# A hosted modulation sum is moved from the first projection phase to the second (fused two-block transformer step)

## What is computed

```python
mod = jax.nn.silu(c) @ w_mod[l] + b_mod[l]
sh1, sc1, ga1, sh2, sc2, ga2 = jnp.split(mod[:, None, :], N_MOD, axis=-1)
p_lat = modulate(rmsnorm(x, g_pre_mix[l]), sh1, sc1) @ w_in[l]
p_ctx = modulate(rmsnorm(ctx, g_pre_mix[l]), csh1, csc1) @ w_in[l]
...
x = x + ga1 * rmsnorm(y_lat, g_post_mix[l])
h_lat = modulate(rmsnorm(x, g_pre_ffn[l]), sh2, sc2)
```

## Time and profile before

| | |
|---|---|
| median of 3 runs | 3192.8 us (3184.38 to 3198.31) |
| span of the profiled execution | 3181.1 us |
| PE busy | 3001.6 us (94%) |
| DVE busy | 2101.7 us (66%) |
| ACT busy | 1289.5 us (41%) |
| POOL busy | 136.9 us (4%) |
| DMA, mean | 185 GB/s |
| first phase's 32 units | about 206 to 358 us |
| differential attention | 361.6 to about 432 us |
| second phase | about 433 to 728 us |

### The profile page before, as it was taken

How to read it: one execution, slowest core, us unless ns; L and a number is a source line. 1 busy time by engine, 2 the same in 40 slices (tenths; PEclk the granted TensorE clock), 3 DMA queues, 4 the chain that set the end, 5 groups by cost and what they waited for, 6 DMA issues and landing times. The chain is left out here.

```text
span 3181.1 us, 42696 instructions
## 1 busy us (share of the span) xinstructions
PE 3001.6 (94%) x16505; PEld 2496.0 (78%) x16505; DVE 2101.7 (66%) x3030; ACT 1289.5 (41%) x2138; POOL 136.9 (4%) x200
## 2 busy tenths in 40 slices
PE   5999889999989999999998999998999999998997
PEld 2577658888779999998887888876757878886766
DVE  5768645746768789887876669545735744774355
ACT  6642334526444444444344323215334224344243
POOL 1000000001010000000001000000010000000000
PEclk9999999999999999999998999999999999999999
DMA  8867224751667777777784546640512644682333
GB/s 269 272 227 270 90 81 140 259 204 35 232 206 259 251 246 258 242 237 271 262 290 155 175 133 201 206 162 14 185 66 100 206 140 139 217 286 73 106 107 138
DMA packets 255577, 589.24 MB, mean 185 GB/s; under 512 B 21977, under 2 KB 30401, under 8 KB 251024
## 3 DMA queue, kind: packets, MB, share of 16 engines
q1 hardware_dynamic: 246336, 546.64, 52.2%
q0 software_dynamic: 8640, 39.22, 3.5%
q10 hardware_dynamic: 400, 0.66, 0.1%
HBM read 571.72 MB, written 14.72 MB: 184 GB/s over the span
## 5 line engine op out<-in xcount | busy, mean ns | idle before, releaser
L2725 DVE TENSOR_TENSOR w_lo<-raw,w_hi 128x1024 fp32r<-128x1024 f32 (+1 forms) x732 | 860.9, 1191 | 395.6 <-ACT w_hi L2704 381.3
L2704 ACT ACTIVATE w_hi<-raw 128x1024 fp32r<-128x1024 f32 (+1 forms) x732 | 741.5, 1032 | 908.1 <-PE bank L2775 514.5
L696 DVE SCALAR_TENSOR_TENSOR acc<-raw,sc_t,acc 128x1024 f32<-128x1024 f32 x480 | 600.9, 1279 | 36.1 <-DMA acc<-in_b_ada 16.1
L2783 PE MATMUL bank<-f_hT_hi,w_hi 128*128 128x256 f32 x1408 | 400.3, 284 | 0.9 <-DVE w_lo L2725 0.9
L2773 PE MATMUL bank<-w_hi,l_hT_hi 128*128 128x512 f32 (+1 forms) x1056 | 391.5, 371 | 8.5 <-DVE w_lo L2725 8.4
L2784 PE MATMUL bank<-f_hT_lo,w_hi 128*128 128x256 f32 x1408 | 399.1, 283 | 0.0
L2785 PE MATMUL bank<-f_hT_hi,w_lo 128*128 128x256 f32 x1408 | 399.1, 283 | 0.0
L2774 PE MATMUL bank<-w_lo,l_hT_hi 128*128 128x512 f32 (+1 forms) x1056 | 388.0, 367 | 0.0
L2775 PE MATMUL bank<-w_hi,l_hT_lo 128*128 128x512 f32 (+1 forms) x1056 | 387.9, 367 | 0.0
L2783 PEld LDWEIGHTS bank<-f_hT_hi,w_hi 128*128 128x128 f32 x1408 | 270.9, 192 | 2.8 <-issue 1.7
L2785 PEld LDWEIGHTS bank<-f_hT_hi,w_lo 128*128 128x128 f32 x1408 | 271.0, 192 | 0.0
(11 more groups left out here) (436 smaller groups left out, 4653.2 us busy)
## 6 DMA issues: line engine op xcount, KB each, us to landing
raw<-in_w_in SPq DMA_DIRECT2D x240, 512.0 KB, 4.9
raw<-in_w_mod SPq DMA_DIRECT2D x192, 512.0 KB, 5.0
raw<-in_w_ada SPq DMA_DIRECT2D x192, 512.0 KB, 4.6
raw<-in_w_up SPq DMA_DIRECT2D x176, 512.0 KB, 4.8
raw<-in_w_out SPq DMA_DIRECT2D x96, 512.0 KB, 5.0
raw<-in_w_down SPq DMA_DIRECT2D x88, 512.0 KB, 5.3
raw<-in_w_in SPq DMA_DIRECT2D x32, 288.0 KB, 3.2
raw<-in_w_ukv SPq DMA_DIRECT2D x16, 512.0 KB, 4.0
```

What stands on the lines that cost most here:

```text
L696: e.scalar_tensor_tensor(acc[a][:, :], raw[s % RAW_SLOTS][:, :], scalar, acc[a][:, :], ALU.mult, ALU.add).then_inc(fma_done, 1)
L2704: e.activation(slot(w_hi[u % SPLIT_SLOTS], g.width), slot(raw[s % RAW_SLOTS], g.width), ACT.Copy).then_inc(hi_ready, 1)
L2725: e.tensor_tensor(slot(w_lo[u % SPLIT_SLOTS], g.width), slot(raw[s % RAW_SLOTS], g.width), slot(w_hi[u % SPLIT_SLOTS], g.width).bitcast(F3 ...
L2783: e.matmul(o, hi[:, kk, c], xh[:, k, 0:n], start=first, stop=False)
```

## The change

One sum group, the first half of `sh2`, leaves the first phase's list and joins the second's. With it the positions of all hosted steps of the two phases change.

```diff
-        gemms([dq1, dk1] + gs[4:6], sums_mix + sums_ffn[0:1], hosts=[(8, 7), (15, 8), (23, 8)], side=(dk_group, drope_dve, 1), then=rows_out, start=start, hooks=hooks)
+        gemms([dq1, dk1] + gs[4:6], sums_mix, hosts=[(9, 10), (20, 11)], side=(dk_group, drope_dve, 1), then=rows_out, start=start, hooks=hooks)
...
-        gemms([mg, mk0, mo0, mk1, mo1, mq0, mq1, mv0, mv1], sums_ffn[1:3], hosts=[(26, 28), (56, 9)],
+        gemms([mg, mk0, mo0, mk1, mo1, mq0, mq1, mv0, mv1], sums_ffn[0:3], hosts=[(10, 20), (32, 16), (52, 14)],
               first=gd_pool, hooks=gates_hooks)
```

## The result

The changed kernel takes 3194.65 us (median of 20 runs, 3191.78 to 3200.8), the kernel before 3188.68 (20 runs, 3180.81 to 3198.31). The ratio is 1.0020 with a 95% interval of 1.0013 to 1.0027: **slower, by some 6.4 us** (the medians differ by 6.0). A second series gave 1.0022 (1.0013 to 1.0031). The profiled execution became 9.4 us longer, 3190.5 against 3181.1.

A forecast was written before the change was run, and what follows sets the result against it. PE was taken to bound both phases. The terms -1.5 + 3.0 - 1.0 + 1.8 + 5.6 + 3.0 - 0.3 gave +10.6 us, from a median of 3192.8 to 3203.4 us; range 3191 to 3215.

The forecast's parts named there:

- The closing one: Whole kernel: the forecast rise of 0.33% lies within the 0.5% (16 us) that a measurement can't tell from no change.
- One stated sign of being wrong: Start of the attention stage: starting earlier than 361.6 us would show the forecast wrong.
- Part 1: Phase 1: 16 sum steps removed relieve DVE, and PE's three listed waits go; -1.5 us, bounds 0 and 2.
- Part 2: Phase 1's end: the barrier waits for the gate rows' stores to land, +3.0 us; row's PE work leaves mid-phase, -1.0.
- Part 3: Phase 2: one more turn of 16 small matmuls on PE between units, with no wait; +1.84 us.
- Part 4: Phase 2, mk0's end: earlier evacuation makes PE wait 3.9 us, then 1.7 us lost at half clock; +5.6 us.
- Part 5: Phase 2, mo1 and mq0: added sum steps make DVE late, +3.0 us in five short waits; -0.3 at mq0's end.
- (a): Rival: mk0's evacuation is hidden after all, so the sum is +5.0, 3197.8 us; chance 0.17.
- (b): Rival: DVE becomes the outright bound of mo1 and mq0, sum 17.3, 3210.1 us; chance 0.18.
- (c): Rival: phase 1 is held by DVE and loads, so removing 16 steps gives -7.1, 3185.7 us; chance 0.05.
- (d): Rival: the placement does nothing measurable anywhere, tail hidden too; -1.0, 3191.8 us; chance 0.05.

The follow-up runs named there:

- e1: The changed kernel with mk0's evacuation put back before weight unit u20, counted in weight units, not list positions; 3188.82 us, ratio 0.9994 to the kernel before.
- e7: The kernel before with mk0's evacuation before weight unit u18 and its later parts one unit sooner than in e3; 3191.48 us, ratio 1.0015.
- e3: The kernel before with only mk0's evacuation moved ahead, to before weight unit u18, hosts as before; ratio 1.0002 to the kernel before.
- e2: e1 with mk1's evacuation put before weight unit u36 too; 3186.2 us, ratio 0.9985 to the kernel before.
- e5: e2 with phase 2's hosted sum steps behind u9-u23, u24-u35 and u56-u64, none in mq0 and mq1; ratio 0.9964, then 0.9977 to the kernel before.
- e4: The changed kernel without POOL's wait for the gate rows' stores at the first phase's end; ACT waits in the attention instead; ratio 1.0012 to the kernel before.

## Why the prediction was wrong

The text called 10.6 us up, and put this within the 0.5% that a measurement can't tell from no change. The time went up by 6.4 us, and with 20 runs the interval excludes "no change". The direction of the sum and the places of its terms were right. Two steps failed. The closing one, that a difference of 0.33% can't be measured, was wrong. And the sum was two thirds too high: the landing of the stores was put too long, the first phase's relief too small and the attention at nothing, while the half clock in mo0 was put too short. The last of these errors has the opposite sign of the others; that it took back 1.7 us of them is luck. One stated sign of being wrong also came true: the attention starts earlier than 361.6, at 358.58. Of these 3.0 us, 1.1 lie in the start part that wasn't changed, and 1.9 are the first phase's -3.4 and +1.5 where the text had -2.5 and +3.0.

- **What can be told.** I took 0.5% from the spread of single runs (3184 to 3198). The interval of the ratio is +-0.07%. A forecast of +0.33% should have been called slower. The forecast time, 3203.4, also stands on a median of three runs, 3192.8, which is 4.1 us above that of twenty.
- **Part 1, phase 1's relief: -1.5 forecast, -2.4 measured** (-3.4 less the 1.0 for the row's sum). The waits listed in the earlier trace rows are not all that late weights cost: PE is shown busy while its modelled matmul ends run into a wait. The count shows it. From 300 to 320 us the kernel before has 80 matmuls (first line below), the changed one 90 (second line); ten matmuls at 0.227 are 2.3 us, where the waits in that stretch give 1.5 (three, the longest 0.7). The starts say the same: around each of the three waits PE lost some 0.26 us more than is listed.

```profile
300.00:320.00 20.00, 18.50 (x80) 14.40 (x79) 19.48 (x21) 4.16 (x5) 0.00 (x0) 1.00 0.82 270
...
300.00:320.00 20.00, 20.00 (x90) 16.57 (x89) 19.12 (x21) 5.10 (x6) 0.00 (x0) 1.00 0.79 248
```

- **Part 2, its end: +3.0 forecast, +1.5 measured**, just under the lower bound of 1.7. The chain was right, step by step: POOL issues the stores 0.29 us behind DVE. The landing was mis-sized. I took 2.56 us behind the issues, and 0.11 for the barrier, from a place in the earlier trace rows where the weight loads ran beside it; measured were 1.14 for both (357.44 to 358.58), so that PE stood idle 3.8 us where the text had about 5. At the end of the phase nothing else is on the queues, and the stores landed 1.5 us from issue:

```profile
DMA packets 64, 0.00 MB, mean 1 GB/s; under 512 B 64, under 2 KB 64, under 8 KB 64
...
gate_rows<-row_out POOLq DMA_DIRECT2D x2, 2.0 KB, 1.5
```

 In the kernel before the same stores took 2.8 us in the stretch from 286 to 292 us, in which the DMA engines moved 234 GB/s, and 3.1 from 331 to 337 us with 347 GB/s; no run here varied the load alone. The end of the range that I had, 1.5, was the nearer row. The Trainium skill ("DMA: Bandwidth & Descriptors", "Anatomy of one DMA — SWDGE (gpsimd) path") gives about 2.0 us as a constant. The measured 1.5 and 2.8 to 3.1 lie on either side of it, and the measurement decides.
- **Part 3: +1.84 forecast, +1.7 measured** in mk1. The turn before u51 waited for nothing, as forecast.
- **Part 4, the early evacuation: +5.6 forecast, +7.3 measured.** Place and mechanism were right, the wait is 4.02 us for 3.9, and e1 and e7 show it by taking it away and by making it alone. What follows it was mis-sized, 3.3 us for 1.7: the stretch at 1.2 GHz was twice as long as the one that I took the price from (6.8 us for 3.4), with fourteen slow matmuls instead of nine: they took 6.14 us where 3.18 would do, and the rest is the 0.26 that a wait costs beside what is listed. Why it was longer stays open, since e3 and e7 show the same 6.8 us behind an idle of 2.88. The Trainium skill ("TensorE: Matmul & The Clock Gate", Part 1) says that idling puts the array at 1.2 GHz; the trace agrees, with a granted clock of 0.50 behind the 4.02 us.
- **Part 5, mo1 to mq1: +2.7 forecast (3.0 - 0.3), +2.7 measured**, by a different split: the 2.51 us wait at u35 was now followed by half clock, and PE, later by that, waited 1.5 us in mq0 (four times 0.38) instead of the five waits of 0.6 to 0.7; in e2, without that half clock, it is 3.0. DVE, which has no idle from 587.59 until behind its last scale at 612.50, set the end. e5 removes it. That half clock alone isn't the +2.7: e3 and e7 have it too, with before's sum steps, and take 74.9 us where the kernel before takes 74.4. The row of the changed kernel:

```profile
584.00:586.00 2.00, 2.00 (x6) 1.57 (x5) 1.84 (x2) 2.00 (x15) 0.00 (x0) 0.50 0.90 302
```

- **Left out: the attention.** The text put nothing down for it, without a reason. Its half-clock stretches lie differently from kernel to kernel and, in the kernel before, from execution to execution. About -1.4 us by the means above, which the scatter doesn't settle.

The sum with the measured terms is +8.2 us against 10.6. Of the rivals, (a), that mk0's evacuation is hidden, (b), slower by DVE outright, (c), faster, and (d), nothing measurable, all failed; the time came out between (a) and the forecast for reasons of size, not because (a) was true.

## What to carry to other kernels

A position counted in steps of a mixed list moves when steps of another kind are put into it; look at every consumer of the list's count before moving anything, and count in the steps that give the cover. Put hosted work behind long units, and not where a short unit already fills the engine that does it. Take the price of a DMA from a place that has the load of the place where it will stand, and let the number of matmuls in a stretch, not the list of waits, say what PE lost.

## What the runs showed of the hardware

In e1 and e2 the clock fell without a recorded idle of PE. It happened during the gates' 8-row transposes, which follow a sum's turn (16 small matmuls, 1.84 us, at 551.19 in e1). Of e1:

```profile
551.00:553.00 2.00, 2.00 (x19) 1.94 (x17) 0.00 (x0) 1.06 (x1) 0.00 (x0) 1.00 0.00 0
553.00:555.00 2.00, 2.00 (x21) 2.00 (x20) 0.24 (x1) 0.00 (x0) 1.43 (x2) 0.61 0.00 0
555.00:557.00 2.00, 2.00 (x6) 1.55 (x7) 1.77 (x7) 0.00 (x0) 0.00 (x0) 0.50 0.05 10
```

mk1 took 50.0 us in both. The changed kernel does the same work in the same order from 557.2 us on, kept a granted clock of 1.00 in both its profiles, as e4 did, and took 46.9. So behind the same two short jobs of small matmuls 3.1 us were lost in two profiles and nothing in three; what decides it isn't shown. e5, whose turn stands at 533, away from the transposes, didn't show it in two profiles. Behind the same idle of 2.5 us the clock stayed up in two profiles of the kernel before and fell in both of the changed kernel and in e1, e3, e4 and e7.
